# Fewer background weight products in attention and in a recurrence: new PSUM layout, joined stages, products placed later

## The reference, cut to what matters

```python
for l in range(DEPTH):                                  # DEPTH = 2
    hx = layer_norm(x) * (1 + sc_x) + sh_x              # the same for ctx with its own modulation
    px_a, px_b, px_c, px_d, px_g = split(hx @ w_in[l])  # px_g: 4 branches x 256 gate columns
    ya = latent attention(px_a)       # 4 heads, softmax(q k^T) v, 1,024 queries against 1,280 keys
    yb = spatial gating(px_b)
    yc = differential attention(px_c) # 4 heads x 2 maps: softmax(q1 k1^T) - lam * softmax(q2 k2^T)
    yd = gated delta rule(px_d)       # both directions, chunks of 64 rows: a recurrence
    acc = sum_i sigmoid(hx @ w_gate[l, i]) * ((y_i * silu(px_g)_i) @ w_branch[l, i])
    x = layer_norm(DEEPNORM_ALPHA * x + gt_x * (acc @ w_out[l])) * ln_g[l] + ln_b[l]
```

## Time and profile before

| | |
|---|---|
| median of the runs | 4619.94 us (4615.93 to 4622.12, 3 runs) |
| profiled execution | 4612.59 us |
| its span | 4610.7 us |
| PE busy | 3656.5 us (79%) |
| DVE, ACT, POOL busy | 2015.9, 1228.7, 1000.9 us |

### The profile page before, as it was taken

How to read it: one execution, slowest core, us unless ns; L and a number is a source line. 1 busy time by engine, 2 the same in 40 slices (tenths; PEclk the granted TensorE clock), 3 DMA queues, 4 the chain that set the end, 5 groups by cost and what they waited for, 6 DMA issues and landing times. The chain is left out here.

```text
span 4610.7 us, 64034 instructions
## 1 busy us (share of the span) xinstructions
PE 3656.5 (79%) x25796; PEld 2830.6 (61%) x25796; DVE 2015.9 (44%) x3493; ACT 1228.7 (27%) x2126; POOL 1000.9 (22%) x1094
## 2 busy tenths in 40 slices
PE   5987888577796999895776877987687977999477
PEld 2764666456574777684662764666466755777365
DVE  4223442256535555413553323441466264554455
ACT  2101220245322323213301202220354132232340
POOL 0001101233103343222400001101332023433150
PEclk7978998789897999998997888999899988999798
DMA  4101001411101111135634101012211112111472
GB/s 168 38 36 36 26 17 50 106 41 37 57 30 55 51 46 51 48 126 163 232 102 167 53 32 45 23 34 81 78 45 39 50 48 63 53 53 42 140 248 91
DMA packets 202042, 334.47 MB, mean 73 GB/s; under 512 B 22688, under 2 KB 96160, under 8 KB 200352
## 3 DMA queue, kind: packets, MB, share of 16 engines
q1 hardware_dynamic: 172960, 283.34, 19.6%
q10 hardware_dynamic: 28800, 47.20, 2.8%
HBM read 249.45 MB, written 81.00 MB: 72 GB/s over the span
## 5 line engine op out<-in xcount | busy, mean ns | idle before, releaser
L89 PE MATMUL ps<-hh,wh_ds 128*128 128x512 f32 (+1 forms) x1600 | 705.6, 441 | 163.6 <-ACT out_ds L182 76.2
L90 PE MATMUL ps<-hl,wh_ds 128*128 128x512 f32 (+1 forms) x1600 | 619.5, 387 | 0.0
L91 PE MATMUL ps<-hh,wl_ds 128*128 128x512 f32 (+1 forms) x1600 | 619.3, 387 | 0.0
L89 PEld LDWEIGHTS ps<-hh,wh_ds 128*128 128x128 f32 x1600 | 325.2, 203 | 253.0 <-ACT out_ds L182 86.5
L195 POOL CAST wh_ds<-raw_ds 128x512 fp32r<-128x512 f32 x160 | 104.7, 654 | 1228.7 <-DMA raw_ds<-in_d_win 400.7
L90 PEld LDWEIGHTS ps<-hl,wh_ds 128*128 128x128 f32 x1600 | 326.2, 204 | 57.7 <-issue 20.0
L91 PEld LDWEIGHTS ps<-hh,wl_ds 128*128 128x128 f32 x1600 | 322.6, 202 | 58.3
L1968 DVE TENSOR_TENSOR T_dr<-T_dr,ps 64x256 f32<-64x256 f32 x400 | 167.6, 419 | 220.1 <-PE ps L1725 210.8
L1137 ACT ACTIVATE qk_da<-ps,nmx_d 128x1280 f32<-128x1280 f32 (+1 forms) x144 | 177.8, 1235 | 300.7 <-DVE nmx_d L1065 259.3
L1866 ACT ACTIVATE TT_dr<-ps 128x512 f32<-128x512 f32 x200 | 117.3, 597 | 398.7 <-PE ps L1715 396.6
L197 POOL TENSOR_TENSOR wl_ds<-raw_ds,wh_ds 128x512 fp32r<-128x512 f32 x160 | 209.7, 1311 | 12.8
(11 more groups left out here) (328 smaller groups left out, 7970.6 us busy)
## 6 DMA issues: line engine op xcount, KB each, us to landing
gate_sums<-out_ds ACTq DMA_DIRECT2D x160, 256.0 KB, 2.0
raw_ds<-in_d_wmerge SPq DMA_DIRECT2D x128, 256.0 KB, 2.7
logit_mg<-gate_sums SPq DMA_DIRECT2D x128, 256.0 KB, 3.4
w_mod<-in_d_wmod SPq DMA_DIRECT2D x12, 2048.0 KB, 20.1
R_dr<-decay_rows SPq DMA_DIRECT2D x80, 256.0 KB, 4.3
q_raw_da<-turned_qk SPq DMA_DIRECT2D x288, 32.0 KB, 1.9
acc_ou<-merged SPq DMA_DIRECT2D x18, 512.0 KB, 5.2
raw_ds<-in_d_win SPq DMA_DIRECT2D x32, 256.0 KB, 2.7
```

The costliest lines, as they stand in the source:

```text
L89: pe.matmul(out, w_hi, x_hi, start=first, stop=False)
L90: pe.matmul(out, w_hi, x_lo, start=False, stop=False)
L91: return pe.matmul(out, w_lo, x_hi, start=False, stop=last)
```

## The change

1. **Recurrence**: no gate groups in it (before 136 in each layer).
2. **attention**: two score regions of three whole banks (0 to 2, 3 to 5); one maximum over all 1,280 columns in place of L1060, L1062 and the join; all transposes in bank 6, in the groups (0,4), (4,4), (8,2), so each group waits until the one before it has been moved; gate groups share bank 7 with the values, and come at four fixed places per query tile with two groups each. That is 8 per tile for all tiles but the first, 56 in the big attentions (before 64 in "a", 128 in "d"), 8 in each small one (before 16 and 32).
3. **`prepare_maps`** takes the place of `rotate_columns` "rd" and `stack_maps`: one phase, 64 groups (before 32 and 48), q is stored after half of the rotations, k is read back in four parts with weight loads between them.
4. **`expand_latents`**: the heads' 64-row outputs are computed in pairs of 128 rows (8 matmuls a chunk, before 14) in 6 banks, and each half is moved by ACT or DVE.
5. **`normalise_rows`**: the low-part subtraction goes from DVE to POOL; weights load and are cut between the row tiles. In the normalise and rotate phases the cuts and loads come two steps later.
6. **`apply_gates`**: three buffers in place of two, each engine's second operation on a piece stands behind the first one of the next piece. All groups left come here: 504 in layer 0 (before 240), 240 in layer 1 (before 8).

```diff
# delta_rule
-    fill.plan(STEPS * POINTS, 1)
+    fill.plan(0, 1)
# attention
-    groups = [(0, 4), (4, 2), (6, 4)] if key_tiles == NT else [(0, CT)]
+    groups = [(at, min(4, key_tiles - at)) for at in range(0, key_tiles, 4)]
+    SPOTS = 4
-    fill.plan(n_tiles * UNITS, rate, (5,))
+    fill.plan((n_tiles - 1) * SPOTS, KD // SPOTS, (7,))
...
+            def scores(h, a):
+                at = 3 * 512 * (h % 2 if maps == 1 else a)
+                return flat[:, at:at + keys]
+            def turn_bank(count):
+                return m.ps[:, 6, 0:count * P]
...
+                    last = u * G + g - 1          # in turn(): the group before, whichever it is
+                    if last >= 0:
+                        movers, moved = (on_act, moved_a) if last % G in on_act else (on_dve, moved_d)
+                        pe.wait_ge(moved, last // G * len(movers) + movers.index(last % G) + 1)
...
+                        if maps == 1:
+                            turns = {0: [0], 1: [1], 2: [2]}
+                        else:
+                            turns = {1: [0], 3: [1], 5: [2]}
+                            for x, (at, width) in enumerate(pieces):
+                                mm = pe.matmul(scores(h, a)[:, at:at + width], ...)
+                                if h == 2 and i and a == 0 and x == 0:
+                                    value(i - 1, 0)
+                                if x == len(pieces) - 1 and a == 0:
+                                    if h == 3 and i < n_tiles - 1:
+                                        spot(i, 1)
+                                    if h == 0 and i:
+                                        spot(i - 1, 2)
+                                    if h == 1 and i:
+                                        spot(i - 1, 3 if maps == 2 else 4)
+                                    for g in turns.get(x + a * len(pieces), ()) if G > 1 else ():
+                                        turn(*before, g)
...
# ACT: before exp of map 0, before exp of map 1, behind it
+                            move(*before, on_act if maps == 1 else on_act[:1])
+                                move(*before, on_act[1:2])
+                        if before and maps == 2:
+                            move(*before, on_act[2:])
# expand_latents
+            for pair in range(HEADS // 2):
+                own = slice(2 * pair * NOPE, 2 * (pair + 1) * NOPE)
+                jobs.append((width, [(wq[:, j, P:][:, own], raw[:, j, cols]) for j in range(2)],
+                             [(q[0:NOPE, 2 * pair + a, cols], halves[a]) for a in range(2)]))
# differential_attention
-        rotate_columns(nc, m, l, "rd", [qk[:, j] for j in range(4)], rate=4)
-            stack_maps(nc, m, l, qk, kk, spare, ...)
+            prepare_maps(nc, m, l, qk, kk, spare.rearrange("p h c -> p (h c)"), ...)
# prepare_maps, SP
+            sp.wait_ge(rotated, 4)
+            sp.dma_start(m.d_qk[:, 0:2], raw[0]).then_inc(q_out, 16)
+            sp.wait_ge(rotated, 8)
+            sp.dma_start(m.d_qk[:, 2:4], raw[1]).then_inc(k_out, 16)
+            for g in range(4):
+                if g >= 2:
+                    sp.wait_ge(k_low, 2 * (g - 1))
+                for n in range(4):
+                    sp.dma_start(raw[g % 2][ROPE * n:ROPE * n + ROPE], src).then_inc(k_in[g % 2], 16)
+                fill.load(sp, 5 + 2 * g)
# normalise_rows: from DVE to POOL
+                    pool.tensor_tensor(m.hl[:, :, t * P:(t + 1) * P], h[:, t % 2],
+                                       m.hh[:, :, t * P:(t + 1) * P].bitcast(F32), ALU.subtract).then_inc(low, 1)
# apply_gates, ACT
+                    act.activation(gate[:, n % SLOTS, 0:width], gate[:, n % SLOTS, 0:width], ACT.Silu).then_inc(silu, 1)
+                    if n:
+                        high(n - 1)
+                    fill.move(act, n - 1)
```

More of the change, by code:

```diff
@@ L129, in upto @@
     def upto(self, point):
-        return self.end if point is None else min(self.end, self.start + point * self.rate)
+        return self.end if point is None else min(self.end, self.start + max(point, 0) * self.rate)
     def bank(self, chunk):
@@ L1072, in _ @@
                         before = earlier(i, h)
-                        if maps == 1 and i and h == LAG:
+                        if i and h == LAG + 1:
                             finish(i - 1)
                         if before:
-                            move(*before, on_dve)
+                            move(*before, on_dve[:1])
+                        for a in range(maps):
+                            find((i * HEADS + h) * maps + a, h, a)
+                            if a == 0 and maps == 2 and (i or h):
+                                mix(*((i, h - 1) if h else (i - 1, HEADS - 1)))
+                        if before:
+                            move(*before, on_dve[1:])
                             if maps == 1:
@@ L1094, in _ @@
                 if maps == 1:
[L1095 to L1096 removed]
+                    keep(i)
+                finish(i)
             @block.scalar
@@ L1197, in _ @@
         def _(pe):
+            pe.wait_ge(table_in, 32)
+            for n, (x, c) in enumerate(steps):
+                at, width = CHUNKS[c]
+                if n >= 2:
+                    pe.wait_ge(with_sin, n - 1)
+                pe.matmul(m.ps[:, n % 2, 0:width], perm, x[:, at:at + width], start=True, stop=True).then_inc(swapped, 1)
+                fill.tensor(pe, n + 1)
             fill.tensor(pe)
@@ L2055, in apply_gates @@
         sb = lambda n, s, d=F32: st.enter_context(nc.sbuf_tensor(f"{n}_ag{l}", s, d))
-        gate = sb("gate", [P, 2, 512])
-        y = sb("y", [P, 2, 512])
-        with phase(nc, "in0", "in1", "silu", "gated", "y_high", "y_low") as (block, in0, in1, silu, gated, y_high, y_low):
-            into = [in0, in1]
+        gate = sb("gate", [P, SLOTS, 512])
+        y = sb("y", [P, SLOTS, 512])
+        with phase(nc, *[f"in{s}" for s in range(SLOTS)], "silu", "gated", "y_high", "y_low") as (block, *sems):
+            into = sems[:SLOTS]
+            silu, gated, y_high, y_low = sems[SLOTS:]
             @block.sync
```

342 lines of the change are left out of this document (167 added, 175 removed).

## The result

The changed kernel takes 4662.64 us in the median (4653.43 to 4666.34, 4 runs), the kernel before beside it 4617.93 us: ratio 1.0095, 95% interval 1.0075 to 1.0116. It is slower by 1%, as forecast in sign. It lies 21 us above the forecast of 4642 and inside the range; as a difference between the two medians, 45 us came where 22 were forecast.

What follows compares the result with a forecast made beforehand. PE was taken to nearly bound the recurrence, a chain of waits attention "d", with groups paying full price in `apply_gates`. Terms of +14 (layer 0) and +8 (layer 1) gave +22, forecast 4642 us, range 4560 to 4720.

Steps and rivals of the forecast that it cites:

- The two largest terms: `apply_gates`: the added gate groups lengthen it by 120 us in layer 0 and 130 us in layer 1.
- the 35 us taken off for hidden pieces: `apply_gates`, layer 0: with three buffers and 504 groups, all but one or two pieces lie beside matmuls, -35 us.
- Rival A: Recurrence: bound by PE alone, small waits don't grow; -80 and -94 instead of -45 and -60, total 4573 us; chance 0.20.
- Rival C: Recurrence: PE at its lower clock level half the time, 84 us a layer, total 4794 us; chance 0.07.
- the chain through ACT's last move and the one bank: Attention "d": next transposes wait for ACT's move behind the second exponential; 7.8 us a head, 34.2 a tile.
- The clock's price of one us a tile: Attention "d": PE is busier at the lower clock with fewer groups, one us a tile, +8 us.
- Rival B: Attention "d": freed by a quicker bank hand-over, -57 and -51 instead of +15 and +20, total 4499 us; chance 0.12.
- attention "a": Attention "a": PE stays the bound, its work falls to 193 us; -20 and -22 us.
- POOL hides them: `normalise_rows`: ten subtractions leave DVE, 12.3 us, and POOL hides all but the last; -8 us a layer.
- the later cuts: Later weight cuts and loads: -3 us a layer.
- the joined stage: Rotation and stacking as one phase: 70 us in place of 88.8, -19; layer 1 -35 us.
- D: Whole kernel: the terms cancel, somewhat more from the recurrence removes the 22 us, total 4622 us; chance 0.12.

Runs made afterwards that it cites:

- e2: The kernel before with one edit, no gate groups in the recurrence: ratio 1.0008 to the kernel before.
- e1: The changed kernel with the 136 gate groups of each layer put back into the recurrence: 4648.79 us, ratio 1.0055 to the kernel before.
- e4: The changed kernel with differential attention's move of the last 256 transposed columns on DVE behind the second maximum, not ACT: 4597.15 us, ratio 0.9941 to before.
- e9: The changed kernel without gate groups in differential attentions, plus five unread matmuls before each transpose lot in two heads of all tiles but the first: ratio 1.0115 to before.
- e8: The changed kernel without any gate group in the differential attentions, big and small: ratio 1.0171 to the kernel before.
- e3: The changed kernel with the low-part subtraction of normalise_rows back on DVE: ratio 1.0087 to the kernel before.
- e7: The changed kernel with weight cuts at the old points in normalise_columns, rotate_columns, normalise_turned, and the old place of loads in normalise_turned: ratio 1.0164 to before.

## Why the prediction was right, and where it was off

The sign and the mechanism of the loss were right: groups moved out of places where they are nearly free into `apply_gates`, where they are not. The two largest terms were off by 5 us or less. The price of a group, 0.588 and 0.69, was right as PE's work for it in the full phase (0.58 and 0.69) and too high at the margin, 0.46 and 0.56; the 35 us taken off for hidden pieces made up for it in the sum. The pieces are hidden mainly by the number of groups: behind the last matmul of layer 0 pass 21 us with 376 groups and two buffers (e2), 17 with 368 and three (e1), and 4 with 504 and three. The third buffer and the new order are worth some 6 us.

The recurrence: 35.4 to 37.2 us a step were measured in layer 0 from the second step on, 35 to 39 forecast. What came back was 0.2 us a group, as taken; the 8 us a layer for the lower clock were not there (0.94 granted in both layers), so it fell by 9 and 14 us more. Rival A is out: PE is idle for 80 us of the phase, and e2 shows the same lengths. Rival C is out: the sixteen matmuls of the earlier trace rows take 428 to 438 ns in two of ten steps in layer 0 and in three in layer 1, in one each before, but PE's work in the phases is 307.8 us, not above the 312 that C took at the upper level.

Attention "d": the chain through ACT's last move and the one bank was right. e4 shows it, and the head of 7.84 us in e9 and the maximum of 1.49 us (1.48 taken before its scaling) meet its terms. The tile was not: it was to take 34 to 36 us and took 37.9 in the mean of layer 1. What was mis-sized is the groups' own share. They were put into the tile with a chunk's move, 0.6 us. But e9, with no groups and the same granted clock as the changed kernel (0.80 and 0.82 against 0.78 and 0.80), has tiles of 34.3 us in the mean and attentions 30 and 28 us shorter, so eight groups cost 3.6 us a tile, 0.5 us each. The clock's price of one us a tile was too small by less: its fall to 0.70 made the tile of e8 1.6 us longer than that of e9. That the tiles of e9 come out at the prediction's 34.2 is luck: they hold no move of a chunk, the lots of values lie beside the chain and lengthen no head of the later tiles, and in their place stand the mix's 0.72 us beside POOL, in three heads of a tile, and one head's 0.55. Also, the terms given for the drain and the clock are 12 us, and +15 and +20 were taken without a word on the rest. Rival B, the freed attention, didn't come.

The steps that failed. First, attention "a": PE's work was to fall to 193 us and its idle time from 29 to 13. In layer 0 PE was busy for 199.9 us and idle for 28. The division by eight tiles hid that the first tile has no groups, and 56 groups in seven tiles are again eight a tile. From one tile's first exponential to the next, tiles with groups took 26.6 to 28.4 us, against 24.9 to 27.7 before. The first tile got shorter, 16.4 against 24.0 us. But all that follows the last tile's first exponential got longer by 6 us, 42 against 36, and the 13 us for start and drain were too few: 7 pass to the first exponential and 19 behind the last one (7 and 15 before). Why the end grew was not tested. Second, `normalise_rows`: "POOL hides them" was wrong, since DVE's normalisation takes twice as long beside POOL's subtraction (e3). Third, the later cuts, mis-sized by a factor of six (e7). Against the forecast the first cost 41 us and the second 23; attention "d" and the joined stage, where I took 70 us for what are 76.5 and 78.7, cost 13 each. The cuts gave back 30, the recurrence 24 and `apply_gates` 7. That is 29 of the 31 us between +22 and the 53 of the profiled pair. So the forecast was near in part by luck: misses of some 90 us one way and 60 the other cancelled.

D, the cancelling of terms, did not come, but its chance of 0.12 was low: the misses of single terms (20 us in several) are as large as the forecast of +22, which is an eleventh of the loss in `apply_gates`, not a seventh.

## What to carry to other kernels

Background work is priced by where it goes, at the margin: here a group cost 0.3 to 0.6 us in a chain with gaps and 0.46 to 0.56 in the phase that takes the rest, so emptying one phase alone changed nothing (e2), and what decides is whether the phase's own chain gets shorter. A shared buffer closes a chain through the slowest of its users: ask behind which instruction its release stands, since one small move that no longer stood behind an exponential was worth 32 to 37 us a layer (e4). Work that waits for a transfer or for a free buffer goes behind the phase's own work on its engine (e7, 32 us). And idle PE time can be dearer than it looks: unneeded matmuls in it won back 9 and 12 us (e9).

## What the runs showed of the hardware

DVE's normalisation of 128 x 1024 took 0.81 us alone and 1.86 us beside POOL's subtraction of the same size, which itself took 2.34 us; with these 12.3 us of DVE work on POOL the phase was 2 to 3 us longer than with them on DVE. And 210 matmuls that nobody needed made attention 9 and 12 us shorter, with the granted clock going from 0.70 to 0.80 and 0.82 and four transposes from 1.09 to 0.63 us in 15 of the 64 lots of layer 1.
